# Four unread products of the unit matrix with 512 columns, ahead of the chunk products of a token-shift layer

## What is computed

```python
def step(state, inp):
    r_t, d_t, k_t, v_t, kk_t, a_t = inp
    sa = jnp.einsum('bhij,bhj->bhi', state, -kk_t)
    state = (state * d_t[:, :, None, :] + sa[..., None] * (kk_t * a_t)[:, :, None, :]
             + v_t[..., None] * k_t[:, :, None, :])
    return state, jnp.einsum('bhij,bhj->bhi', state, r_t)
_, y = lax.scan(step, jnp.zeros((b, RWKV_HEADS, RWKV_HEAD_DIM, RWKV_HEAD_DIM), f32), xs)
```

## Time and profile before

| | |
|---|---|
| median of 3 runs | 1779.69 us |
| the three runs | 1772.58, 1779.69, 1804.97 us |
| the profiled execution | 1770.94 us |
| its span, first to last instruction | 1769.1 us |
| mean granted TensorE clock | 0.981 |
| TensorE matmul busy | 1697.9 us |

### The profile page before, as it was taken

The page is one execution under the profiler, slowest core; times in us unless marked ns, Lnnn a source line. Parts: engine busy times, 40 slices in busy tenths (PEclk is TensorE's granted clock), DMA queues, the critical chain, the costliest instruction groups (busy, mean ns, idle before and its releaser), DMA issues.

```text
span 1769.1 us, 26216 instructions
## 1 busy us (share of the span) xinstructions
PE 1697.9 (96%) x10726; PEld 1325.5 (75%) x10726; DVE 1029.3 (58%) x1988; ACT 423.3 (24%) x1052; POOL 259.9 (15%) x339
## 2 busy tenths in 40 slices
PE   8999999999999999999888999999999899999998
PEld 8997487775799849996366778699946677566774
DVE  4777435743477737777457857377663454524463
ACT  2000114532210102100136322310002254222531
POOL 3333000000022201221002212022200220002100
PEclk9999999999999999999989979999999999999999
DMA  8666744212455455555523310345456783457830
GB/s 262 216 212 207 170 107 139 73 48 95 133 163 182 169 171 161 159 176 178 167 77 117 110 49 1 96 143 183 151 183 134 105 147 102 95 82 116 147 112 24
DMA packets 196966, 237.25 MB, mean 134 GB/s; under 512 B 28300, under 2 KB 177216, under 8 KB 196592
## 3 DMA queue, kind: packets, MB, share of 16 engines
q1 hardware_dynamic: 191872, 224.97, 45.6%
q0 software_dynamic: 4960, 10.61, 2.0%
q10 hardware_dynamic: 16, 0.00, 0.0%
HBM read 232.30 MB, written 1.07 MB: 132 GB/s over the span
## 4 chain that ended last, share of the span: by engine, by line
PE 90%; DVE 5%; ACT 3%; DMA 1%; issue 1%; POOL 0%; DVEq 0%; SPq 0%; POOLq 0%; ACTq 0%
PE ps L584 28%; PE ps L277 24%; PE ps L650 14%; PE ps L518 6%; PE ps L594 3%; PE ps L1864 2%; PE ps L1695 1%; DMA arena<-arena 1%; PE ps L2412 1%; PE ps L2424 1%; PE ps L335 1%; PE ps L2443 1%; PE ps L2438 1%; PE ps L1881 1%; PE ps L1893 0%
## 5 line engine op out<-in xcount | busy, mean ns | idle before, releaser
L277 PE MATMUL ps<-hT,ring 128*128 128x272 f32 (+4 forms) x1696 | 360.4, 368 | 4.3 <-ACT hT L359 4.0
L277 PEld LDWEIGHTS ps<-hT,ring 128*128 128x128 f32 (+1 forms) x1696 | 288.7, 191 | 58.4 <-issue 8.3
L584 PE MATMUL ps<-arena,ring 128*128 128x128 f32 x1280 | 162.5, 275 | 0.0
L650 PE MATMUL ps<-ring,arena 128*128 128x512 f32 x352 | 155.9, 593 | 1.7 <-DVE more L755 1.7
L842 POOL TENSOR_TENSOR arena<-arena 128x128 f32<-128x128 f32 x44 | 36.6, 833 | 793.4 <-DVE arena L769 449.6
L584 PEld LDWEIGHTS ps<-arena,ring 128*128 128x128 f32 x1280 | 152.6, 192 | 0.0
L584 PE MATMUL ps<-hT,ring 128*128 128x128 f32 x1280 | 150.1, 275 | 0.0
L584 PEld LDWEIGHTS ps<-hT,ring 128*128 128x128 f32 x1280 | 146.5, 192 | 0.0
L650 PEld LDWEIGHTS ps<-ring,arena 128*128 128x128 f32 x352 | 66.6, 190 | 87.2 <-issue 87.2
L584 PE MATMUL ps<-arena 128*128 128x128 f32 x960 | 120.3, 275 | 0.0
L584 PEld LDWEIGHTS ps<-arena 128*128 128x128 f32 x960 | 113.6, 192 | 0.0
(11 more groups left out here) (482 smaller groups left out, 2716.3 us busy)
## 6 DMA issues: line engine op xcount, KB each, us to landing
ring<-in_ffn_w_gate SPq DMA_DIRECT2D x44, 1024.0 KB, 5.4
ring<-in_ffn_w_up SPq DMA_DIRECT2D x44, 1024.0 KB, 7.1
ring<-in_ffn_w_down SPq DMA_DIRECT2D x44, 1024.0 KB, 5.0
ring<-in_w_in SPq DMA_DIRECT2D x32, 1024.0 KB, 10.1
ring<-in_ab_w_in SPq DMA_DIRECT2D x12, 1024.0 KB, 5.3
ring<-in_w_out SPq DMA_DIRECT2D x8, 1024.0 KB, 4.9
ring<-in_ab_w_out SPq DMA_DIRECT2D x6, 1024.0 KB, 4.9
ring<-in_c_w_k SPq DMA_DIRECT2D x4, 1024.0 KB, 6.3
```

Of the source, the lines that this page charges most:

```text
L277: last = nc.tensor.matmul(o, l, r, start=(i == 0), stop=(i == len(pairs) - 1))
L584: m = nc.tensor.matmul(o, left[:, k, :], right[:, k, :], start=(k == 0), stop=(k == 3))
L650: return nc.tensor.matmul(ps[:, BANK[i], :], hid[p][:, left, :], right, start=(p == 0), stop=(p == LAST))
```

## The change

Between the drain behind `bonus_rows` and the first chunk products, TensorE now issues four products of `ident` with the first 512 columns of `cst`. All four write the same ScalarE bank, the one that the first L1893 product will take next (its number is computed, not taken, so all later numbers stay as they are). No semaphore is raised by them and nothing reads what they write. Ahead of them stands the wait that the first L1893 product has for that bank.

```diff
             bonus_rows()
             pe.drain().then_inc(slot_used, 1)
             s += 1
+            n = pe_a.n + 1
+            pe.wait_ge(act_out, n - 4)
+            for i in range(4):
+                group(bank_a(n), [(ident, cst[:, 0:512])])
             for t in range(T):
                 chunk_pe(pe, t, turn_a, turn_d)
```

## The result

| | before | after |
|---|---|---|
| median | 1773.69 us (20 runs) | 1782.45 us (20 runs) |
| lowest, highest | 1768.43, 1804.97 | 1776.51, 1789.90 |
| profiled execution, its span | 1770.94, 1769.1 | 1784.91, 1783.1 |
| mean granted clock | 0.981 | 0.979 |

The ratio of the times is 1.0041, with a 95% interval of 1.0022 to 1.0061: 7.3 us slower, 3.9 to 10.8. The ratios leave out executions over 1.5% above the fastest of their kernel, but still count most of the kernel before's executions of 1790 to 1798 us, whose cause the experiments are about.

The account below looks back on a forecast made before the run. The prediction took TensorE's own work to bound the kernel: four products cost 5.61 us, a high clock at the scores gives back 1.36, net +4.25 on 1776.1, so 1780.4 us. The range was 1770.94 to 1796 us.

Parts of the forecast that it names:

- What bounds the kernel: Whole span: TensorE, busy for 96% of it and 90% of the last chain; work inserted there lengthens the kernel.
- rival (d): Behind the change: the loss is absorbed later, total 1776.1 us; chance 0.05.
- Price of the four products: Ahead of the scores: 2.21 products at 1.83 us, 1.79 at 0.873 us, together 5.61 us.
- Delay of the rise: From the start of the new products to the clock's rise: 4.05 us taken, from delays of 3.4 to 5.95.
- What is given back: Scores to the second masked group, at the high clock from the start: 4.12 us instead of 5.48, saving 1.36 us.
- Net at the place: New products through the second masked group: 5.61 less 1.36, +4.25 us; forecast range +2 to +5.5 us, chance 0.70.
- The total: Whole kernel: 1776.1 us, the median of four executions, plus 4.25 gives 1780.4 us.
- Rival (a): At the new products: they don't shorten the low clock at all; net +7.3 us at most, 1783.4 us; chance 0.12.
- Rival (b): Chunk products: clock at 0.5 through most of them, 53 us lost with the four products, 1829 us; chance 0.02.
- Rival (c): Chunk products: slower runs' longer low clock is ended by the new products; faster or level, 1775.2 us; chance 0.08.

Follow-up runs that it names:

- late_four: Against the kernel before: the same four unread products, placed behind the chunk products and ahead of the transposes of the result; median 1777.95 us, ratio 0.9965 to 1.0036.
- two_gates: Kernel before with chunk 1's two gate products moved from before the solving to between bonus transposes and scores, no unread products; median 1780.01 us, ratio 0.9987 to 1.0077.
- two_gates_split: As two_gates, but the second solving step waits for ScalarE's copies only ahead of its second chunk; median 1779.14 us, ratio 0.998 to 1.0078 to the kernel before.
- before_again: The kernel before, unchanged, run and profiled a second time; median 1775.40 us, ratio 0.998 to 1.0046.
- pause_three: Kernel before with three unread products in TensorE's pause before the second solving step, none before the scores; median 1795.81 us, ratio 1.001 to 1.0135.
- thin_four: The changed kernel with its four unread products using 32 rows in place of 128; median 1784.13 us, ratio 0.9957 to 1.0036 to the kernel before.

## Why the prediction was right

- **What bounds the kernel.** Right: TensorE's work is the chain, and the insertion was paid at its place. No wait hid it, and at the first product with `w_o` the changed kernel was 4.2 us later (1116.8; 1116.9 had been forecast), so rival (d), a loss absorbed later, was not seen.
- **Price of the four products.** 5.61 us forecast; 6.47 and 5.53 in the two profiles. With the delays measured there the prediction's own prices give 6.43 and 5.45, so the delay made the difference. The price of one product at the low clock was a little high, without effect: 1.83 us from L518, whose six rows hold some 0.37 us at their start beside the products. In the changed kernel the weight loads of the unread products stand 0.85 us apart at the low clock, two to a product, so 1.71. At the high clock 0.85 to 0.87, as forecast.
- **Delay of the rise.** I took 4.05 us; 5.6 and 3.7 us were measured, both within the 3.4 to 5.95 that I gave. The delay is not a property of the place: it differs between executions of one kernel. The Trainium skill ("TensorE: Matmul & The Clock Gate", Part 1, "What's actually happening") warns that the cold stretch varies from run to run; the traces agree, 3.7 and 5.6 us for the same four products. The rule that the prediction took from that section of the Trainium skill, that the warm-up is a stretch of time whichever products fill it, is not what these runs show: 7.2 us of thin products, and in another execution 49.9 us of chunk products, passed at 0.5.
- **What is given back.** 4.12 us forecast for the scores to the second masked group at the high clock, 4.09 measured, by the very chain that was worked out (0.92, through VectorE's 1.01, 0.66, 0.87, 0.59). The 1.36 us given back depend on the kernel before, though: its 5.48 us were 6.6 in its second profile.
- **Net at the place.** +4.25 forecast; +5.1 and +4.1 measured against the first profile.
- **The total.** 1780.4 forecast, 1782.45 measured. That these are only 2 us apart is in part luck: the start, 1776.1 us from four executions, was 2.4 us above the median of twenty, 1773.69, and the change from it, +4.25, was below the measured one. The difference to before was 8.8 us in the medians of the first comparison and 4.3 in the second. The excess of the first, some 3 us by the ratio and 4 to 5 by the executions under 1790 us, is not explained; in the profiled pair it was the fetches from DRAM, and those scatter without the change too ("later" is 656.5 and 664.2 us for the kernel before, 659 to 666 with wide products ahead of the scores).
- **Rival (a)**, that the products don't shorten the low clock: not seen with these products in three profiles; seen with thin ones in their one profile, 7.2 us at 0.5.
- **Rival (b)**, the clock at 0.5 through most of the chunk products: I gave it 2 in 100 and held against it that the same products had got the high clock within 4.05 us in the trace before. That was one execution. Something like it happens in about one execution of four of the kernel before, and cost 21 us where it was profiled, not the 53 that I worked out: at the low clock TensorE no longer waits for VectorE (40.00 us busy of 40, against 46.48 of 50 in the earlier trace rows), and in that execution the second chunk had the clock back. Where it lasted through both chunks, behind the thin products, the first product with `w_o` came 44.8 us later than in the earlier trace rows. It did not happen in 32 executions of the changed kernel.
- **Rival (c)**, that the spread of before is the clock in the chunk products and the new products end it: its mechanism is right and I had said that nothing ties the spread to this place. Its price was wrong: it moves the long executions and not the median, since most executions of before get the clock back by themselves.

## What to carry over

A median can hide half of what an insertion does: this one costs 4 to 5 us at its place in each execution and takes away a loss of some 21 us that hits one in four, and in the mean of all executions the two kernels were 4.1 us apart in the first comparison and 0.6 us the other way in the second. In this kernel thin products of the same length brought nothing. A few wide ones spread over the small solving products gained 5.7 us in one comparison (1770.94 us), against a loss of 1.1 to 9.0 us with wide ones in front of the scores (both by the executions under 1790 us), but with a ninth one added the gain did not come again. A ratio over executions of two kinds needs the same care: count how many of each kind it holds. Before giving a rival 2 in 100 because the trace shows otherwise, take the spread of the timed runs as a sign that a second trace may not.

## What the runs showed of the hardware

- TensorE was busy at every us of a stretch of 40 us, and in another kernel of 96 us, with the granted clock at 0.5 all the time. A busy TensorE does not mean 2.4 GHz.
- Four products of 512 columns over 128 rows were followed by the rise of the clock 3.6 to 5.6 us after their start in three of three profiles (one of them with eight), and two of them after 3.7 to 3.8 in two of two; four over 32 rows were not in their 7.2 us (one profile), nor were four of 128 and 32 rows in turn in 8.0 us (two profiles).
- The same chunk products, started at the low clock, had the high clock after 3.2 to 4.05 us in three profiles (the first of before, `late_four`, `two_gates`), after 15.2 us in `two_gates_split`, and after 49.9, 52.3 and 97.4 us in `before_again`, `pause_three` and `thin_four`. Once at the high clock they kept it in all profiles but one (46.48 us busy of 50 at 1.00 in the earlier trace rows). The one fall seen among them came where TensorE waited for VectorE, and other profiles have the same wait without a fall. What decides whether they regain or lose the clock in an execution is open.
- The fetch of the cumulated rows from DRAM (L2621 before, two per execution) took from 5.8 to 12.1 us from issue to landing, over the fourteen profiles, with or without unread products.
